# The delta rule's scan: gate rows spread by DMA, the inverse applied once, a chunk's front part made during the chunk ahead of it

## The reference, cut to what matters

```python
gcum = jnp.cumsum(gc, axis=-1)
diff = gcum[..., :, None] - gcum[..., None, :]
kb = kc * bc[..., None]
a = -jnp.einsum('bhid,bhjd->bhij', kb, kc) * jnp.exp(jnp.where(strict, diff, -jnp.inf))
rhs = jnp.concatenate([kb * jnp.exp(gcum)[..., None], vc * bc[..., None]], axis=-1)
sol = lax.linalg.triangular_solve(eye - a, rhs, left_side=True, lower=True, unit_diagonal=True)
w, u = sol[..., :dk], sol[..., dk:]
v_new = u - w @ s
attn = jnp.einsum('bhid,bhjd->bhij', qc, kc) * jnp.exp(jnp.where(incl, diff, -jnp.inf))
o = (qc * jnp.exp(gcum)[..., None]) @ s + attn @ v_new
s_new = jnp.exp(g_last)[..., None] * s + jnp.einsum(
    'bhjd,bhje->bhde', kc * jnp.exp(g_last - gcum)[..., None], v_new)
```

## Time and profile before

| | us |
|---|---|
| three timed runs: median | 4615.59 |
| lowest, highest | 4613.99, 4621.42 |
| the profiled execution's own time | 4620.74 |
| its span in the trace | 4618.9 |
| PE busy in the span | 4180.4 (91%) |
| DVE, ACT, POOL busy | 1547.1, 937.9, 625.1 |

### The profile page before, as it was taken

One profiled execution on the slowest core, in us unless ns is written; L12 is line 12 of the kernel. 1 busy time (PEld: TensorE's weight loads), 2 busy tenths in 40 slices (PEclk: granted clock), 3 DMA queues, 4 the chain that ended last, 5 costly groups with the idle time before them and its releaser, 6 DMA issues.

```text
span 4618.9 us, 52458 instructions
## 1 busy us (share of the span) xinstructions
PE 4180.4 (91%) x21742; PEld 2643.8 (57%) x21742; DVE 1547.1 (33%) x3411; ACT 937.9 (20%) x1764; POOL 625.1 (14%) x635
## 2 busy tenths in 40 slices
PE   6997888888889899999999989889989999799899
PEld 3477787475545654444444446777555557685454
DVE  2664444222423511111111254452045153631351
ACT  4122222122110012000000241132035220221341
POOL 3002323003100211000000220221000100311001
PEclk7997788895688899999999999999999999899999
DMA  5200000213132621111111030221010030311100
GB/s 198 81 5 2 2 2 5 89 44 118 65 104 85 219 91 46 37 37 46 37 37 37 32 119 28 77 70 59 28 42 24 27 124 28 96 46 54 50 24 37
DMA packets 197371, 271.10 MB, mean 59 GB/s; under 512 B 7773, under 2 KB 157488, under 8 KB 196240
## 3 DMA queue, kind: packets, MB, share of 16 engines
q1 hardware_dynamic: 183792, 199.08, 13.9%
q0 software_dynamic: 13344, 68.66, 3.9%
HBM read 232.95 MB, written 34.77 MB: 58 GB/s over the span
## 4 chain that ended last, share of the span: by engine, by line
PE 85%; DVE 7%; issue 3%; ACT 2%; DMA 2%; POOL 1%; SPq 0%; DVEq 0%; POOLq 0%; ACTq 0%
PE ps L789 15%; PE ps L2569 10%; PE ps L2583 10%; PE ps L2479 8%; PE ps L811 7%; PE ps L3238 5%; PE ps L3520 3%; PE ps L2237 2%; PE ps L1348 2%; PE ps L3731 1%; PE ps L2281 1%; PE ps L835 1%; PE ps L3714 1%; DMA big<-hs_scratch 1%; PE ps L1362 1%
## 5 line engine op out<-in xcount | busy, mean ns | idle before, releaser
L789 PE MATMUL ps<-big 128*128 128x512 f32 (+1 forms) x1760 | 685.3, 551 | 15.2 <-DMA big<-hs_scratch 15.2
L789 PEld LDWEIGHTS ps<-big 128*128 128x128 f32 x1760 | 336.4, 192 | 353.9 <-issue 344.8
L2569 PE MATMUL ps<-big 128*128 128x512 f32 x1024 | 442.2, 594 | 8.6 <-issue 8.6
L2583 PE MATMUL ps<-big 128*128 128x512 f32 x1024 | 440.8, 593 | 0.0
L2479 PE MATMUL ps<-big 128*128 128x512 f32 (+1 forms) x896 | 359.3, 563 | 3.0 <-DVE big L3849 2.0
L2633 DVE SCALAR_TENSOR_TENSOR big<-ps,big 128x512 f32<-128x512 f32 x128 | 96.1, 751 | 776.6 <-PE ps L2583 776.6
L2569 PEld LDWEIGHTS ps<-big 128*128 128x128 f32 x1024 | 195.6, 191 | 253.7 <-issue 253.7
L2583 PEld LDWEIGHTS ps<-big 128*128 128x128 f32 x1024 | 195.0, 190 | 244.5 <-issue 244.5
L811 PE MATMUL ps<-big 128*128 128x256 f32 (+1 forms) x1792 | 319.2, 342 | 12.5 <-DVE big L1789 10.2
L811 PEld LDWEIGHTS ps<-big 128*128 128x128 f32 x1792 | 288.8, 195 | 43.5 <-DVE big L1789 10.3
L2479 PEld LDWEIGHTS ps<-big 128*128 128x128 f32 x896 | 170.0, 190 | 187.3 <-issue 180.5
(11 more groups left out here) (461 smaller groups left out, 5564.7 us busy)
## 6 DMA issues: line engine op xcount, KB each, us to landing
big<-in_w_mlp SPq DMA_DIRECT2D x32, 1024.0 KB, 5.2
big<-in_w_in SPq DMA_DIRECT2D x29, 1024.0 KB, 5.1
big<-in_w_mod SPq DMA_DIRECT2D x24, 1024.0 KB, 5.4
big<-in_w_ada SPq DMA_DIRECT2D x24, 1024.0 KB, 6.4
big<-us_scratch SPq DMA_DIRECT2D x72, 256.0 KB, 4.5
hs_scratch<-big POOLq DMA_DIRECT2D x3, 5120.0 KB, 14.9
big<-c_dft SPq DMA_DIRECT2D x12, 1024.0 KB, 5.5
xs_scratch<-big POOLq DMA_DIRECT2D x16, 640.0 KB, 3.8
```

The source lines that it names most:

```text
L789: t = e.matmul(b[:, 0:n], wv[:, k, 128 * m:128 * m + 128], K.hT[:, k, t0:t0 + n], start=(k == 0), stop=(k == 7))
L2569: t = e.matmul(b[:, :], wv[:, k, 128 * m:128 * m + 128], K.hT[:, k, t0:t0 + n], start=(k == 0), stop=(k == 7))
L2583: t = e.matmul(b[:, :], wv[:, k, 128 * m:128 * m + 128], h[:, k, t0:t0 + n], start=(k == 0), stop=(k == 3))
```

## The change

- The gate rows no longer go through PE. When they are ready in `GdnProj`, POOL's DMA queue writes them to DRAM (`K.us`), and in the scan SP issues for every chunk a DMA that reads one chunk's row (four heads x 128) into all 128 partitions of a new SBUF buffer `gc` of the chain. It waits until the chain's previous user of the buffer is through. `decay` on DVE and `qe` on ACT read `gc` from SBUF.
- w is not made any more. PE multiplies keys by the state (`old`, L1466), DVE multiplies that by the negated decay `egc` and adds the values (L1623), and PE applies the inverse once to the result (`new`, L1477). POOL's key scaling L1291, PE's L1378 and ACT's L1463 go.
- The steps stand in an order of their own. A chunk's `decay` is made by DVE in step left 5 of the chunk two places ahead of it in the chain, its `triangle` (kk, exponentials, `LT`) after that chunk's level 6, its first mask in that chunk's `old`. The masks for level n + 1 are issued with left n; the product of `qe` and queries moves from a chunk's front to left 5; the scores (`queries`) come after level 2.

```diff
-    def chains(self, steps):
+    def chains(self, make):
...
+        def run(d, q):
+            s = make(d, q)
+            s.decay(q)
+            yield
+            s.triangle(q)
+            yield
+            for place in range(q, 10, 2):
+                more = place + 2 < 10
+                s.first(place)
+                yield
+                for n in range(1, 7):
+                    s.left(place, n)
+                    if n == 5 and more:
+                        s.decay(place + 2)
+                    yield
+                    s.right(place, n)
+                    yield
+                    if n == 2 and GDN_ORDER[d][place] < 8:
+                        s.queries(place)
+                        yield
+                if more:
+                    s.triangle(place + 2)
+                yield
+                while st[d] < place:
+                    yield
+                s.old(place)
+                yield
+                s.new(place)
+                yield
+                s.state(place)
+                st[d] = place + 1
+                yield
...
+        e.wait_ge(*self.at("gdn rows away"))
+        for place in range(10):
+            for d in range(2):
+                c = GDN_ORDER[d][place]
+                if place >= 2:
+                    b = GDN_ORDER[d][place - 2]
+                    e.wait_ge(*self.at(*self.key("DT", d, b)))
+                    if b < 8:
+                        e.wait_ge(*self.at(*self.key("qe", d, b)))
+                L = self.lane(f"gdn_rows{d}{place % 2}_in")
+                e.dma_start(m.chain[d, place % 2]["gc"], K.us[0, d, c].partition_broadcast(128)).then_inc(
+                    L.sem, L.up(self.key("rows", d, c), by=16))
...
+    def new(self, place):
+        e, P, d, c, ch = self.e, self.P, self.d, self.chunk(place), self.ch
+        u = self.key("vn", d, c)
+        b = self.pr.open(e, u)
+        e.wait_ge(*self.at(*self.key("X", d, c, 6)))
+        e.wait_ge(*self.at(*self.key("XF", d, c)))
+        e.wait_ge(*self.at(*self.key("rest", d, c)))
+        for h in range(4):
+            t = e.matmul(b[:, 96 * h:96 * h + 96], ch["XF"][:, 128 * h:128 * h + 128], ch["vn"][:, 96 * h:96 * h + 96],
+                         start=True, stop=True)
+        t.then_inc(P.sem, P.up(("mm", u)))
...
+    def old(self, place):
+        e, V, m, d, c, vn = self.e, self.V, self.m, self.d, self.chunk(place), self.ch["vn"]
+        u = self.key("old", d, c)
+        e.wait_ge(*self.at("mm", u))
+        for h in range(4):
+            sl = slice(96 * h, 96 * h + 96)
+            e.scalar_tensor_tensor(vn[:, sl], self.bank(u)[:, sl], m.egc[:, c, 4 * d + h:4 * d + h + 1], m.vtm[:, c, sl],
+                                   ALU.mult, ALU.add).then_inc(V.sem, V.up(self.key("rest", d, c), ("free", u, 0)))
```

624 lines of the change are left out of this document (308 added, 316 removed).

## The result

The changed kernel takes 4557.55 us (median of four runs, 4540.76 to 4570.61) where the kernel before takes 4618.51 in the same comparison (4613.99 to 4626.26): a ratio of 0.9864, with a 95% interval from 0.9829 to 0.99. It saves 61 us where 123 were forecast, and lies outside the range. The profiled execution took 4558.8 us.

The account below looks back on a forecast made before the run. PE was taken to bound the scan, losing 86 us idle and 46 to the low clock. Work 293, idle 31 and low clock 19 gave a 343 us scan instead of 466, median 4493 us, range 4475 to 4535.

Parts of the forecast that it names:

- the low clock: Scan, PE at 1.2 GHz instead of 2.4: costs 19 us after the change, 9 of it at the start; 46 before.
- somewhere after: Scan after its start: PE work at the low clock costs 10 us more.
- rival 1: Scan: the low clock stays, costing 40 instead of 19; scan 364, median 4514; chance 0.17.
- The prediction's own signs: Scan checks: end near 683, PE busy 305 to 320, first product near 350, mean clock 0.9 or more.
- (e): DVE's bursts from `old`: PE waits 1.7 at `new`, 0.5 allowed for the decay burst; 17 us in all, between 0 and 36.
- (d): Gate rows by DMA: 4.5 us a read, hidden after the start; first product at 350.5 instead of 348.2.
- rival 2: DVE's bursts decide, colliding with POOL at 0.2 to 0.4 more per instruction; scan typically 365, median 4516; chance 0.14.
- (c): Idle time at a chunk's front goes where the front is made ahead; it stays at the scan's start.
- The idle time: PE idle in the scan: 10 at the start, 17 in bursts, 4 at the end, 31 us.
- (a): PE no longer spreads gate rows (gc) in the scan: 20 x 1.09 = 22 us off its work.
- (b): w is no longer made on PE in the scan: 20 x 0.95 = 19 us off its work.
- The work: PE's work in the scan at the high clock: falls from 334 to 293 us.

Follow-up runs that it names:

- e1_fill: Changed kernel plus unneeded 128x128 products where PE waits: seven ahead of left 6, five ahead of left 2 (direction 0, even chunks); 4537.46 us.
- e9_three: Changed kernel with `qe` product in left 6, direction 1's decay a step later than direction 0's, ScalarE's `XF` copies in right 6; 4509.21 us.
- e11_three_warm_fill: e10_three_warm plus six unneeded 128x128 products ahead of `new` of direction 0 in the even chunks; 4494.13 us.
- e5_pe_rows: e2_qe_later with gate rows spread by TensorE into PSUM again, read there by DVE and ScalarE, no rows DMA; 4536.64 us.
- e2_qe_later: Changed kernel with POOL's product of `qe` and queries in step left 6 instead of left 5; 4537.11 us.
- e6_spread: e2_qe_later with direction 1's decay made one step later than direction 0's; 4525.99 us.
- e4_once: Kernel before with only `old` and `new`: no w, no key scaling, no copy of w; 4622.98 us, ratio 1.0008.
- e12_rows_by_pe_warm: Changed kernel with gate rows by TensorE instead of DMA, `qe` and `XF` copies moved one step, unneeded products at the scan's start; 4516.14 us.
- e15_dense_left5: e10_three_warm plus four unneeded 128x128 products ahead of left 5 of sixteen chunks; 4535.52 us.
- e10_three_warm: e9_three plus 34, 10 and 16 unneeded 128x128 products ahead of the first products of the first three chains; 4513.12 us.

## Why the prediction was wrong

**The step that failed** is the low clock, "somewhere after, 10, together 19". It cost 71 us: 52 of the 59 us by which the stretch of 402 is longer than the forecast 343. Split by the time for which PE is busy at the low clock, at the prediction's own factor of 1.7, the start up to 400 us took 15 of the 9 forecast (37 us busy), and the "somewhere after" took 54 of the 10 forecast (132 us busy): this is the term that was mis-sized. The prediction let most of the falls go with the gaps at a chunk's front, and its argument against rival 1 was that 574 to 594 "held 1.00 through all the small waits between groups". Such a stretch doesn't show what a wait of 1.96 or 1.34 us does, which the change leaves in mid-stream, and the same stretch has 0.73 now. The longest low stretch in the steady part of the kernel before was 24 us; those of 34 us with PE full are new. e1_fill, e9_three and e11_three_warm_fill show the term by filling or removing the waits: the excess of PE's busy time over the 293 falls from 71 to 22 in e9_three. The prediction's own signs said as much: PE busy for 364 us and not 305 to 320, and a mean clock that stayed near 0.8.

**Rival 1** had the right mechanism and little over half its price. It took the low clock in proportion to the work, 46 x 293 / 334 = 40. But the price goes with the time for which PE is busy at the low clock, and that rose by half although the work fell, from 112 to 169 us: at 1.7 these are 46 and 69, the two excesses that the traces show. With the gaps at the front gone, a low stretch has nothing left to hide in. The 1.7 itself, from small products, is a little low for scores, `old` and `new` (3.50 against 1.85 us, 1.9 times).

**(e), the bursts.** That of `new` was right: L1477 waits for L1623, 1.91 us at 466.5, against 1.7 forecast, but only once in the changed kernel and not once a round; where the clock is low, PE itself takes so long that DVE is ready first (543.90). The decay burst was wrong: "2 x 1.8 on DVE, has 3.7 us of right products to catch up in; I allow 0.5". It is 6.9 us long and PE waits 1.96. In the same prediction stood the rule on shared interfaces, weighed against (d) and priced at 0.2 to 0.4 for an instruction (rival 2), worked out from masks of 0.7 us beside L1529. Beside two `qe` products the price is the rest of both: 2.18 us for one instruction. The change moves exactly these products into left 5, next to the decay; the prediction had the one in (c) and the other in (d), and did not put the two timelines beside each other. e5_pe_rows shows it: with the decay reading PSUM and nothing else spread, the wait is gone. e2_qe_later only moves the collision and leaves 1.69 us of the wait, and e6_spread removes it by splitting the burst, though three L1560 (the decay's minimum) take 2.61 us there beside `qe`.

**The idle time** was about right in sum, 38 against 31. (c) holds: L1410 waits 18.0 us in all, only at the start. That is 8 more than the 10 forecast, since the q = 1 chains have a start of their own:

```profile
350.33 1.12 PE L1410 MATMUL ps<-big 64*64 64x64 f32 x16 [9.56 <-POOL big L1665]
...
354.56 1.12 PE L1410 MATMUL ps<-big 64*64 64x64 f32 x16 [3.12 <-POOL big L1665]
...
388.73 1.12 PE L1410 MATMUL ps<-big 64*64 64x64 f32 x16 [5.29 <-POOL big L1665]
```

**(d)** held where it was measured in time: first product at 350.33 (350.5 forecast), one wait of L1556 for the DMA, 1.7 us, at the start. **(a)** is true of PE's work and worth nothing in the time against e5_pe_rows: 22 us off PE against a DVE that is slowed by POOL. **(b)** alone gives nothing either (e4_once, forecast as -19 with the front hidden); with the front ahead it wasn't tried.

**The work**, 293, seems some 8 us too high. e11_three_warm_fill and e12_rows_by_pe_warm have the clock high nearly throughout, so they show it best. From their busy time, 320 and 327, I take the unneeded products (90 and 60 at 0.27 us, 24 and 16), in the second the rows' 22, and what 27 and 10 us of busy time at the low clock cost at 1.7 (11 and 4). That leaves 285 in both, an estimate. By it the low clock cost the changed kernel nearer 79 us than 71.

**What stays open**: why the clock comes back within 4 us in some places and after 34 in others; why it passed waits of 1.9 us in e12_rows_by_pe_warm and e15_dense_left5, and fell behind waits of 0.64 in e1_fill and e5_pe_rows; and why the same unneeded products at the start held it up in e10_three_warm and not in e15_dense_left5. That the waits bring it down is shown by what filling them does, over all, and not at each wait. That `qe` and decay collide because both read SBUF rests on the rows (L1526 beside `qe` before) and on e5_pe_rows, where the decay reads PSUM and keeps its 419 ns.

## What to carry to other kernels

In a stream of small products, cost a wait of 0.6 to 2 us on TensorE not by its length but by the clock that it may take with it: here up to 34 us at half clock stood behind one, and three moves of work by one step each, with none removed, were worth 48 us. Price the low clock by the time for which TensorE is busy in it: where an edit removes idle time, the low clock that stays costs more than before. When an edit makes an engine read SBUF instead of PSUM, and another moves a long GpSimd instruction, lay the two timelines over each other before pricing either. And work taken off the busiest engine counts only once the wait that sets its pace is gone.
